# Output products of a two-layer decoder kernel: retention before attention, and one more piece of SBUF for early expert weights

## The reference

```python
ret = retention(rq, rk, rv, rg)                  # (256, 2048)
att = dsa_attention(aq, ak, av, iq, ik, iw)      # (256, 1024)
merged = sigmoid(gr) * (ret @ w_ret_o) + sigmoid(ga) * (att @ w_dsa_o)
h = layer_norm(ALPHA * x + merged @ w_out)
# HierMoE: each token goes to one of 4 groups and to 2 of the 8 experts in it
y = (silu(h_e @ w_gate[e]) * (h_e @ w_up[e])) @ w_down[e]   # 32 experts
x = layer_norm(ALPHA * h + weighted sum of its two experts' y)
```

## Time and profile before

| What | Value |
|---|---|
| time, median of 3 runs | 1599.21 us (1599.19 to 1601.15) |
| span of the profiled execution | 1597.9 us; some 1.3 us of a run lie around it |
| TensorE matmul busy | 1302.9 us (82%) |
| VectorE busy | 619.6 us (39%) |
| ScalarE busy | 394.1 us (25%) |
| DMA, both layers | 524.60 MB, mean 328 GB/s |
| DMA while the experts run | 424 to 430 GB/s in nearly every slice of 40 us, mean busy share 9 tenths or more |
| DMA while the mixer runs | 121 to 305 GB/s |

### The profile page before, as it was taken

How to read it: one execution, slowest core, us unless ns; L and a number is a source line. 1 busy time by engine, 2 the same in 40 slices (tenths; PEclk the granted TensorE clock), 3 DMA queues, 4 the chain that set the end, 5 groups by cost and what they waited for, 6 DMA issues and landing times. The chain is left out here.

```text
span 1597.9 us, 21422 instructions
## 1 busy us (share of the span) xinstructions
PE 1302.9 (82%) x8690; PEld 882.5 (55%) x8690; DVE 619.6 (39%) x1065; ACT 394.1 (25%) x458; POOL 0.2 (0%) x4
## 2 busy tenths in 40 slices
PE   9999999999756656657799999999997556556667
PEld 8998889995312212212298988899943122212212
DVE  6788676655100100100287876865541001000102
ACT  3334734333100000001143357343320000000011
POOL 0000000000000000000000000000000000000000
PEclk9999999999978877878899999999999778788779
DMA  8455446689999999999964454366999999999996
GB/s 305 166 194 190 163 159 216 246 351 424 426 429 427 428 428 427 428 427 428 404 223 164 159 211 170 121 247 233 397 427 426 427 424 428 425 429 427 429 425 276
DMA packets 98903, 524.60 MB, mean 328 GB/s; under 512 B 5504, under 2 KB 9984, under 8 KB 71184
## 3 DMA queue, kind: packets, MB, share of 16 engines
q1 hardware_dynamic: 98080, 523.10, 81.3%
q10 hardware_dynamic: 752, 0.50, 0.1%
HBM read 522.53 MB, written 1.05 MB: 328 GB/s over the span
## 5 line engine op out<-in xcount | busy, mean ns | idle before, releaser
L1057 PE MATMUL psum<-ring,aqT 128*32 128x512 f32 x1440 | 261.9, 707 | 114.0 <-PEq L1045 114.0
L1823 DVE TENSOR_TENSOR w_low<-ring,w_high 128x2048 fp32r<-128x2048 f32 (+2 forms) x108 | 239.8, 2260 | 70.8 <-DVEq L1822 69.4
L1331 ACT ACTIVATE w_high<-ring 128x2048 fp32r<-128x2048 f32 (+2 forms) x108 | 198.7, 1887 | 194.8 <-ACTq L1327 178.4
L1057 PE MATMUL psum<-spare,aqT 128*32 128x512 f32 x256 | 131.0, 701 | 96.3 <-PEq L1158 96.3
L2059 DVE TENSOR_TENSOR qk<-psum,qk 128x512 f32<-128x512 f32 x16 | 11.1, 692 | 481.6 <-DVEq L2058 481.6
L1057 PEld LDWEIGHTS psum<-ring,aqT 128*32 128x32 f32 x1440 | 66.9, 128 | 213.2 <-issue 213.2
L1057 PE MATMUL psum<-rv,tmp 128*32 128x512 f32 x240 | 123.1, 703 | 69.8 <-PEq L1185 69.8
L734 PE MATMUL psum<-x_high,w_high 128*128 128x256 f32 x512 | 146.8, 287 | 0.0
L734 PE MATMUL psum<-x_high,w_low 128*128 128x256 f32 x512 | 143.3, 280 | 0.0
L734 PE MATMUL psum<-x_low,w_high 128*128 128x256 f32 x512 | 143.2, 280 | 0.0
L637 PE MATMUL psum<-w_high,x_high 128*128 128x512 f32 (+2 forms) x352 | 138.7, 394 | 0.0
(11 more groups left out here) (285 smaller groups left out, 2301.4 us busy)
## 6 DMA issues: line engine op xcount, KB each, us to landing
ring<-in_w_gate_dram SPq DMA_DIRECT2D x56, 2048.0 KB, 33.0
ring<-in_w_in_dram SPq DMA_DIRECT2D x34, 2048.0 KB, 7.9
ring<-in_w_up_dram SPq DMA_DIRECT2D x28, 2048.0 KB, 21.8
spare<-in_w_up_dram SPq DMA_DIRECT2D x14, 2048.0 KB, 14.3
rv<-in_w_down_dram SPq DMA_DIRECT2D x12, 2048.0 KB, 31.1
rg<-in_w_down_dram SPq DMA_DIRECT2D x12, 2048.0 KB, 35.5
x_xT<-in_w_down_dram SPq DMA_DIRECT2D x12, 2048.0 KB, 39.9
ring<-in_w_down_dram SPq DMA_DIRECT2D x12, 2048.0 KB, 29.0
```

What stands on the lines that cost most here:

```text
L1057: mm = nc.tensor.matmul(bank[s, :], lhs[:, c, s], w[:, k, n * NB:(n + 1) * NB], start=(c == 0), stop=(c == chunks - 1))
L1331: nc.scalar.activation(half_tile(high, i % HIGH, w, b), half_tile(ring, i % RAW, w, b), ACT.Copy).then_inc(high_ready, 1)
L1823: V.tensor_tensor(half_tile(low, i % RAW, w, b), half_tile(ring, i % RAW, w, b), half_tile(high, i % HIGH, w, b).bitcast(f32), ALU.subtrac ...
```

## The change

The retention's four products come first and the attention's two after them. `outputs` becomes `retained_outputs` (no tile by halves any more) and `attended_outputs`, whose second tile, dsa1, is now the one that is done by halves. `merged_high` still lies in `att_high`'s place, which dsa1 reads now at the last place: so ScalarE's `merged_split_high(0)` moves behind the first half of `split_high(LAST)`, which waits for dsa1's lower half to be done. `h` loses its buffer: its first row block goes to `tmp`, the second to `x[:, 0, :]`; x gets a buffer of its own and is no home any more; its transpose and the gates with the merged sums share `xT_sums`, whose halves are the homes `xT` and `sums`. `hidT` moves out of `tmp` to the place of the attention's keys and values, the parameter rows to `x[0:8, 1]`, and `load_params` to behind `first_gathered`. The lists of homes follow.

```diff
-OUT_TILES = ["dsa0", "dsa1", "ret00", "ret01", "ret10", "ret11", "out0", "out1"]
+OUT_TILES = ["ret00", "ret01", "ret10", "ret11", "dsa0", "dsa1", "out0", "out1"]
...
-EARLY = [(10, "spare0", "rg0"), (11, "spare1", "rg0"), (23, "table", "gr0"), (16, "rv1", "dsa0"),
-         (2, 10, "ret00"), (1, "stage", "ret01"), (3, 11, "ret10"), (18, "rg0", "out1"),
-         (22, "qk0", "out1")]
-FIRST = [(6, 2, "ret11"), (0, "qk1", "mid"), (7, 3, ""), (19, "rg1", ""), (17, "rv0", "rv"),
-         (8, 4, "out00"), (12, 6, ""), (4, 0, "out10"), (14, 8, ""), (9, 5, "out01"),
-         (13, 7, ""), (5, 1, "out11"), (15, 9, ""), (20, "x1", "x1"), (21, "x0", "x0")]
+EARLY = [(10, "spare0", "rg0"), (11, "spare1", "rg0"), (23, "table", "gr0"), (16, "rv1", "ret00"),
+         (2, 10, "ret10"), (1, "stage", "ret11"), (18, "rg0", "dsa1"), (22, "qk0", "dsa1"),
+         (0, "qk1", "out0"), (19, "rg1", "out0")]
+FIRST = [(6, 2, "dsa1"), (3, 11, "mid"), (7, 3, ""), (17, "rv0", "rv"), (8, 4, "out00"), (12, 6, ""),
+         (4, 0, "out10"), (14, 8, ""), (21, "sums", ""), (9, 5, "out01"), (13, 7, ""), (5, 1, "out11"),
+         (15, 9, ""), (20, "xT", "xT")]
...
-        x_xT = sb("x_xT", [P, 2 * TT * D])
-        x = x_xT[:, 0:TT * D].rearrange("p (t n) -> p t n", t=TT)
-        xT = x_xT[:, TT * D:].rearrange("p (k s) -> p k s", k=KC)
-        h = sb("h", [P, TT, D])
+        x = sb("x", [P, TT, D])
+        xT_sums = sb("xT_sums", [P, 2 * TT * D])
+        xT = xT_sums[:, 0:TT * D].rearrange("p (k s) -> p k s", k=KC)
...
-        h_flat = h[:, :, :].rearrange("p t n -> p (t n)")
+        h_flat = xT_sums[:, TT * D:]
...
+        h = [tmp_flat, x[:, 0, :]]
...
-        hidT = tmp_flat[:, 0:512].rearrange("p (j s) -> p j s", j=FC)
+        hidT = ak_av[:, :].rearrange("p (j s) -> p j s", j=FC)
...
-        param_rows = tmp_flat[0:8, NB:2 * NB]
+        param_rows = x[0:8, 1, 0:NB]
...
                 for n in range(2):
-                    turned(f"dsa{n}", four(f"DO{n}"), (att_high, att_low), done={3: f"DO{n}"})
-                copied("RT3", "RO0x")
+                    retained_outputs(n)
                 for n in range(2):
-                    outputs(n)
+                    attended_outputs(n)
                 count_and_gather(out_and_logits())
...
@@ ScalarE
-                load_params(l)
                 router_weights(l)
                 for i in range(21, LAST - 1):
                     split_high(i)
+                split_high(LAST - 1)
+                split_high(LAST, (0,))
                 merged_split_high(0)
-                split_high(LAST - 1)
-                split_high(LAST)
+                split_high(LAST, (1,))
                 merged_split_high(1)
...
                 first_gathered()
+                load_params(l)
...
@@ VectorE
                 dve.wait_ge(gates_in, 4).then_inc(gates_in, -4)
-                for n in range(2):
-                    ps = take(f"DO{n}").rearrange("p b (a s) -> p (b a) s", s=SEQ)
-                    c = slice(4 * n, 4 * n + 4)
-                    step(V.tensor_tensor(gaT[:, c, :], gaT[:, c, :], ps, ALU.mult))
-                    free(f"DO{n}")
-                    split_low(22 + n)
-                    if n == 0:
-                        fold_norm()
+                fold_norm()
+                split_low(22)
+                gated("RO0x", 0)
+                gated("RO0y", 2)
+                split_low(23)
                 centre_router()
                 split_low(24)
-                gated("RO0x", 0)
-                free("RO0x")
-                gated("RO0y", 2)
-                free("RO0y")
+                gated("RO1x", 4)
+                gated("RO1y", 6)
+                split_low(25)
+                gated_attention(slice(0, 4), take("DO0"))
+                free("DO0")
                 merge(0)
-                split_low(25)
+                split_low(LAST - 1)
                 merged_rest(0)
-                split_low(LAST - 1)
                 split_low(LAST, (0,))
-                gated("RO1x", 4)
-                free("RO1x")
-                gated("RO1y", 6)
-                free("RO1y")
+                for b in range(2):
+                    gated_attention(slice(4 + 2 * b, 6 + 2 * b), take("DO1")[:, b:b + 1, :])
+                free("DO1")
                 merge(1)
```

More of the change, by code:

```diff
@@ L82 @@
 FIRST_HOME = {u: home for u, home, _ in EARLY + FIRST}
-OUTSIDE = ["rg0", "rg1", "qk0", "qk1", "rv0", "rv1", "x0", "x1", "spare0", "spare1", "table", "stage"]
+OUTSIDE = ["rg0", "rg1", "qk0", "qk1", "rv0", "rv1", "sums", "xT", "spare0", "spare1", "table", "stage"]
 assert sorted(FIRST_HOME) == list(range(6 * QUAD))
-PLACES = [5, 0, 1, 2, "spare", 3, 4, None, "rv", "rg", "x", 5]
+PLACES = [5, 0, 1, 2, "spare", 3, 4, None, "rv", "rg", "xT_sums", 5]
 APART = 2 * QUAD - 1
@@ L94 @@
 Taq1a Prk1v Prv1a RS0v Prv2a AS0v RS1v Prv3a AT0a AS1v Prg0a AO0a AT1a AS2v Prg1a AO1a AT2a AS3v
-Prg2a AO2a AT3a RY0v Prg3a AO3a RY1v Pgr0a RT0a RY2v Pgr1a RT1a RY3v Pga0a RT2a Pga1a RT3a DO0v DO1v
-RO0xv RO0yv RO1xv RO1yv OUT0v OUT1v HT0a RLv""".split()
+Prg2a AO2a AT3a RY0v Prg3a AO3a RY1v Pgr0a RT0a RY2v Pgr1a RT1a RY3v Pga0a RT2a Pga1a RT3a RO0xv RO0yv
+RO1xv RO1yv DO0v DO1v OUT0v OUT1v HT0a RLv""".split()
 JOB = {j[:-1]: n for n, j in enumerate(JOBS)}
@@ L237, in build @@
         high = split("w_high", ring, RAW * TILE, [P, HIGH, TILE])
-        x_high = split("x_high", x_xT, TT * D, [P, KC, SEQ])
+        x_high = split("x_high", xT_sums, 0, [P, KC, SEQ])
         x_low = split("x_low", ring, (RAW + HIGH) * TILE, [P, KC, SEQ])
@@ L536, in _ @@
                             load_first(l * NE, u)
-                frees = dict(ret11=ret_used, mid=mid_free, rv=rv_free, x0=x0_free, x1=x1_free,
+                frees = dict(dsa1=dsa_used, mid=mid_free, rv=rv_free, xT=xT_free,
                              out00=out_used[0, 0], out10=out_used[0, 1],
@@ L753, in turned_by_halves @@
                             for m, (a, v) in enumerate(((wh, xh), (wl, xh), (wh, xl))):
-                                mm = nc.tensor.matmul(out, a[:, k, c], v, start=False,
-                                                      stop=(k == KC - 1 and m == 2))
+                                mm = nc.tensor.matmul(out, a[:, k, c], v,
+                                                      start=(b % 2 == 0 and k == 0 and m == 0),
+                                                      stop=(k == KC - 1 and m == 2),
+                                                      skip_group_check=True)
                                 if b == 0 and k == 0:
@@ L758, in turned_by_halves @@
                                 if b == 0 and k == KC // 2 and m < 2:
-                                    mm.then_inc(ret_used if m else high_used, 1)
+                                    mm.then_inc(dsa_used if m else high_used, 1)
                         if half == 1 and b in done:
@@ L778, in outputs, with attended_outputs @@
                 turned(f"ret{n}0", outs, [v[:, 0:KC, :] for v in (ret_high, ret_low)], stop=False,
-                       first={3: gw_ready} if n == 0 else {})
-                upper = [v[:, KC:, :] for v in (ret_high, ret_low)]
-                done = {1: f"RO{n}x", 3: f"RO{n}y"}
+                       first={3: gw_ready} if n == 1 else {})
                 if n == 0:
-                    turned(f"ret{n}1", outs, upper, start=False, done=done)
-                else:
-                    turned_by_halves(f"ret{n}1", outs, upper, done)
+                    copied("RT3", "RO0x")
+                turned(f"ret{n}1", outs, [v[:, KC:, :] for v in (ret_high, ret_low)], start=False,
+                       done={1: f"RO{n}x", 3: f"RO{n}y"})
+            def attended_outputs(n):
+                outs = four(f"DO{n}")
+                if n == 0:
+                    turned("dsa0", outs, (att_high, att_low), done={3: "DO0"})
+                    return
+                turned_by_halves("dsa1", outs, (att_high, att_low), {1: "DO1", 3: "DO1"})
             def out_block(out, t, n, terms, columns=slice(0, NB), began=None):
@@ L989, in first_gather @@
                 for k in chunks:
-                    mm = nc.tensor.matmul(first_xg[k], h[:, t, k * P:(k + 1) * P], pick[:, t, :],
+                    mm = nc.tensor.matmul(first_xg[k], h[t][:, k * P:(k + 1) * P], pick[:, t, :],
                                           start=(t == 0 and k < 4), stop=(t == TT - 1),
@@ L1001, in gather @@
                     for t in range(TT):
-                        mm = nc.tensor.matmul(wide_y[:, k * P:(k + 1) * P], h[:, t, k * P:(k + 1) * P],
+                        mm = nc.tensor.matmul(wide_y[:, k * P:(k + 1) * P], h[t][:, k * P:(k + 1) * P],
                                               pick[:, t, :],
```

39 lines of the change are left out of this document (21 added, 18 removed).

## The result

The changed kernel takes **1607.51 us** (median of 5 runs, 1606.31 to 1610.62) against 1599.21 beside it: a ratio of 1.0050, 95% interval 1.0039 to 1.0061, 8.3 us slower. I had said 1596.6 and a range up to 1600.3. The profiled execution has a span of 1605.6 us, 7.7 more than before.

What follows compares the result with a forecast made beforehand. The DMA engines were taken to bound the layer's end. A cap of 2.8 (2.9) us a layer less a 1.55 us stall gave 2.65 us over both layers: median 1599.2 to 1596.6 us, range 1593.3 to 1600.3.

Steps and rivals of the forecast that it cites:

- The cap, 2.8 us a layer: Before the second quad's first matrix: backlog 10.4 - 7.6 us, the most that bytes moved earlier can win.
- what is won stays won to the layer's end: Behind the second quad's first matrices: landings bound the stage, each later issue follows a landing, so the gain persists.
- The stall at S(7): At TensorE's first product with w_out: a 1.55 us wait per layer for the rounding chain behind out1's landing.
- rival (b): At place 7: out1 lands late, at up to 10.4 us; stall 4.1 us, 1.3 lost a layer, 1601.9 us; chance 0.1.
- Carried over whole: From place 7 to the second quad's first issue: TensorE's whole 1.55 us delay passes on, 35.3 of 35.4 us being work.
- Units go out at S(4) and S(5), share near 0.9: At places 4 and 5: SP issues qk and rg units there, bringing the DMA share near 0.9.
- nothing is owed at S(7): At the start of place 7: eleven units done, no transfer outstanding, where before about 1.4 us more was owed.
- small gaps: At the waits `out01` and `out11`: less in the queue, gaps of some 1 us, part of 3.3 us given back.
- one unit and a third: In the queue behind the start of place 7: this much transfer, 3.3 us a layer, is taken off.
- Places 1 to 5, and the parameters: New order at places 1 to 5 costs nothing; four parameter DMAs, issued near 375 us, nothing, at most 0.5 us a layer.
- the bound of 1602.4: Whole kernel: a measured time over 1602.4 us counts as slower; chance 0.08.
- (c): At the second quad's first matrix: a 9.1 us landing is the rule, cap 1.3, eaten by the stall; 1599.7 us; chance 0.15.

Runs made afterwards that it cites:

- the second profile: The changed kernel run again, word for word, beside others on the same chip: 1606.86 us, ratio 1.0042.
- the old order with the late rounding: Kernel before, with only ScalarE's and VectorE's new order: first merged half rounded behind the first half of split_high(LAST); 1605.67 us, ratio 1.0036.
- the kernel with three units less and the shorter products: Kernel before without DMAs of units 19, 17 and 21, and without the third term in the upper half of the w_out products; 1594.67 us, ratio 0.9968.
- the kernel with the rounding first: Changed kernel with ScalarE's rounding of the first merged half put ahead of the gates' half that waits for out1; 1600.65 us, ratio 1.0001.
- the kernel with three units less: Kernel before without the DMAs of units 19, 17 and 21, products reading other units' places; 1600.43 us, ratio 0.9999.

## Why the prediction was wrong, point by point

**The cap, 2.8 us a layer: failed, what is won by it is 0.** This is the larger error, 5.7 us of the sum. I took 10.4 - 7.6 as a backlog that could be given up. The kernel that gave up 7.35 us of transfer landed the matrix 8.3 us behind its issue, so the floor was 8.3 and not 7.6 (a figure of w_out tiles that I had called "if anything long"), which leaves 2.1. Of the 2.1 another 1.1 went at the second matrix, which TensorE lets go just as late and which again finds nothing in front of it. The rest went at single landings later on, for a reason that stays open. The step that failed is "what is won stays won to the layer's end". I read it from idle weight loads; that row names no landing as what ended the idle time ("issue" stands for a wait that the profile doesn't explain), and even a stage bound by landings doesn't show that a lead at its start survives. What the runs showed in its place: bytes taken off the queue alone give 0 (1.0001 and 0.9999), because TensorE's path ends at the same issue; with that path shorter too, 4.8 to 5.2 us come out.

The Trainium skill, page "DMA: Bandwidth & Descriptors", section "Anatomy of one DMA — SWDGE (gpsimd) path", whose fit is for DMAs that GpSimd issues and not SP, would give 6.8 us for this matrix. The measured 8.3 decides, and it is farther from it than the 7.6 of the tiles was. By that figure the cap would have been larger still, and the miss too.

**The stall at S(7): the mechanism was right, the size short.** 1.55 us forecast, 2.14 and 1.90 measured, 1.96 and 2.27 in the second profile (start from S(6), less 10.83). out1 landed after 8.25 us and not 7.8, +0.45: its DMA follows two busy places, as rival (b) had it, mostly far from its 10.4, but 10.2 in one layer of one run. The rest, in layer 1, is 0.15 us in the hand-overs. The half (1.92), the rounding (1.04) and `merged_rest` (1.23) took what I had written. Unit 17, which waits for `rv_free`, was issued 17.9 us behind S(6) for 17.7 forecast (`merge(1)` at 343.29), and from 339.82 on TensorE is busy for 36.94 of 36.99 us: the later `merged_rest(1)` was covered. "Carried over whole" held: a delay of 0.8 to 0.9 us a layer already shows in the time.

**The clock: not in the sum.** In two profiles of the changed kernel, one of the two stalls in each was followed by 3.4 us at half clock, 1.5 us more on the path. I had written that TensorE's work of 35.3 us would follow unchanged. Of the two stalls in the old order with the late rounding neither was followed by it, so not each stall brings it: two of six. The two are those with the longest idle times, 1.87 and 2.00 us; the other four were idle for 1.42 to 1.70. But length alone doesn't tell it either: in the kernel with three units less and the shorter products 3.4 us at half clock followed an idle time of 0.4 us.

**The rest of the loss.** Stalls of 2.14 + 1.90 and one half clock of 1.5 make 5.5 us of the 8.3 (interval 6.2 to 9.8). In the profile the second quad's first matrix is issued 3.7 and 1.9 us later, lands 3.3 and 0.6 later, and the layer's last down matrix 4.9 and 1.8 later. So the earlier transfers did win 0.4 and 1.3 us at the first landing, and 1.6 and 1.2 us were lost behind it, most of them in steps at single landings like those above (0.9 us at the eleventh matrix of layer 1, 1.1 at the sixth of layer 2, 0.6 at the thirtieth of both). That is the account of one execution. Over all runs delays cost more than their length in two (+3.2 for 1.8, +5.7 for 3.5) and not in three others (+4.6 for 4.4, +7.7 for 8.2, +8.9 for 8.0). What part of the excess is chance is open.

**The queue.** "Units go out at S(4) and S(5), share near 0.9" was right (0.94, 0.96), and so was "nothing is owed at S(7)". I had placed "small gaps" at the waits of out01 and out11; the gap is at S(7) itself, since only unit 6 is issued between out1 and the first product: 3.5 us at 0 GB/s with the stall; without it, in the kernel with the rounding first, the 5.2 us behind S(7) still go at 232 GB/s (403 before). The bytes moved to places 4 and 5 come out of this stretch. In that kernel the last unit lands 2.0 us earlier than before in one layer and 1.0 in the other, where "one unit and a third" was 3.3 us.

**Places 1 to 5, and the parameters: right.** With the rounding first everything else of the change is there and costs 0.2 us by the ratio (within 1.4); the two medians differ by 0.7. The four parameter DMAs take ScalarE 1.55 us from 377.70 on, as forecast, and TensorE's matmuls on them begin at 389.87 with no gap. The rule that I had cited from the Trainium skill (page "DMA: Bandwidth & Descriptors", section "Queues, rings and completion order") says that a DMA engine takes turns among the queues. The trace agrees: between 377 and 383.7 us, before the first of the sixteen marks (383.79) of the matrix that SP had issued ahead at 376.81, five packets of ScalarE's queue (q10) stand among SP's (q1; packets, MB, share):

```profile
q1 hardware_dynamic: 192, 2.31, 93.7%
q10 hardware_dynamic: 5, 0.01, 0.3%
```

**The rivals.** (b) named the right place and the right sign, with a price of 4.1 - 2.8 a layer; with nothing won by the cap, a stall of 1.6 us a layer is enough for slower by the bound of 1602.4. (c) saw that the floor might be higher than 7.6, but let the cap end at 1.3. No rival had the cap at nothing: the chance of 0.08 for slower hung on what no row of before shows: what becomes of a lead when TensorE's issues come as late as ever.

## What to carry to other kernels

Before costing a gain of one resource, ask what the other one does at the same point: where two limits meet, either alone can be worth nothing, a delay of the one that was tried here (TensorE) is paid whole, and only an experiment that eases both shows that there is a gain. A backlog of one transfer in front of a DMA is not all slack to be spent: it is what the engines move while the packets of the next issue are on their way, and without it two dips of 3 us cost 1.0 MB here. A lead at one landing has to be followed to the last. And an in-order operation put behind a wait for a landing (here a rounding of 1 us behind a gates' half) should be costed with every hand-over and with the clock behind the idle time.

## What the hardware showed that I had not expected

- A 2 MB matrix of 16 KB pieces into a nearly empty queue took 8.2 to 8.3 us from issue to landing, where w_out's tiles, in smaller pieces, took 7.6 to 7.9 in most layers of the old order.
- In the windows of 30 us that moved only 389 to 406 GB/s the DMA engines were busy for 0.97 to 1.00, against 1.01 at 427 to 429: their busy share hides most of the loss, GB/s shows it.
- A landing can fall back by 0.6 to 1.6 us in its last mark alone, with other matrices queued ahead of it; in the kernel with three units less, layer 1, the whole matrix had lost the lead ten matrices on.
- After idle times of 1.4 to 2.0 us TensorE went to half clock for 3.4 us in two of six cases, the two longest; in four cases with matmuls on scrap data in the wait it never did.
